# Memory keys and queries transposed inside the gate chunk, head queries behind the values, branch rows split earlier

## The reference

```python
for i in range(DEPTH):
    h = rmsnorm(x, norm_in[i])
    z = h @ w_in                       # queries, keys, values, q_mem, gate
    mix = mla_mixer(...) if i % 2 == 0 else swa_mixer(...)
    mem_o = memory_attention(q_mem, mem, ...)   # 4 heads of 128
    branch = concatenate([mix, mem_o]) * silu(gate)    # 1024 + 512 wide
    x = x + branch @ w_out[i]
```

## Time and profile before

| | |
|---|---|
| median of 3 runs | 1450.37 us (1449.27 to 1455.12) |
| the profiled execution | 1454.06 us, span 1452.3 us |
| TensorE busy | 1399.7 us, 96% |
| VectorE busy | 982.6 us, 68% |
| ScalarE busy | 760.7 us, 52% |
| GpSimd busy | 412.5 us, 28% |
| DMA | 121.47 MB, mean 84 GB/s |
| mean granted TensorE clock | 0.995 |

### The profile page before, as it was taken

One profiled execution on the slowest core, in us unless ns is written; L12 is line 12 of the kernel. 1 busy time (PEld: TensorE's weight loads), 2 busy tenths in 40 slices (PEclk: granted clock), 3 DMA queues, 4 the chain that ended last, 5 costly groups with the idle time before them and its releaser, 6 DMA issues.

```text
span 1452.3 us, 23072 instructions
## 1 busy us (share of the span) xinstructions
PE 1399.7 (96%) x8120; PEld 1242.3 (86%) x8120; DVE 982.6 (68%) x2072; ACT 760.7 (52%) x1823; POOL 412.5 (28%) x535
## 2 busy tenths in 40 slices
PE   7999999999999999999999999999999999999999
PEld 6889889898888988889878898899888888888997
DVE  6455688887755546888564657887877556477873
ACT  7354466555544436666462535656556344366651
POOL 2221342331202123645211213322311211245450
PEclk9999999999999999999999999999999999999999
DMA  6313221114341322213352132121133413122222
GB/s 231 108 47 88 82 61 53 44 47 145 127 121 50 87 63 66 69 56 97 96 194 83 45 94 82 46 61 46 37 116 116 117 44 98 57 70 62 63 72 102
DMA packets 88673, 121.47 MB, mean 84 GB/s; under 512 B 10352, under 2 KB 58864, under 8 KB 88560
## 3 DMA queue, kind: packets, MB, share of 16 engines
q1 hardware_dynamic: 83088, 112.31, 25.6%
q10 hardware_dynamic: 5472, 7.69, 1.7%
HBM read 115.77 MB, written 4.19 MB: 83 GB/s over the span
## 4 chain that ended last, share of the span: by engine, by line
PE 70%; DVE 14%; ACT 8%; issue 4%; POOL 2%; DMA 1%; SPq 1%; ACTq 0%; DVEq 0%; POOLq 0%
PE bank L1499 21%; PE bank L1501 21%; PE bank L1500 21%; PE bank L1543 5%; ACT prob L574 3%; DVE w_lo_t L873 3%; DVE bank L1260 3%; DVE probT L881 2%; POOL rr L1330 1%; ACT w_hi L549 1%; DVE gate L928 1%; PE bank L1505 1%; PE bank L1506 1%; DMA w_raw<-in_w_mem 1%; ACT q_st L571 1%
## 5 line engine op out<-in xcount | busy, mean ns | idle before, releaser
L873 DVE TENSOR_TENSOR w_lo_t<-w_raw,w_hi 128x256 fp32r<-128x256 f32 (+3 forms) x540 | 301.0, 574 | 306.1 <-ACT w_hi L549 293.8
L549 ACT ACTIVATE w_hi<-w_raw 128x256 fp32r<-128x256 f32 (+3 forms) x544 | 268.1, 510 | 353.4 <-PE bank L1501 331.3
L1499 PE MATMUL bank<-w_hi,actT 128*128 128x256 f32 (+3 forms) x1120 | 363.1, 324 | 7.3 <-DVE qT L883 3.6
L1500 PE MATMUL bank<-w_lo_t,actT 128*128 128x256 f32 (+3 forms) x1120 | 360.3, 322 | 0.0
L1499 PEld LDWEIGHTS bank<-w_hi,actT 128*128 128x128 f32 x1120 | 213.8, 191 | 23.5 <-DVE qT L883 4.1
L1500 PEld LDWEIGHTS bank<-w_lo_t,actT 128*128 128x128 f32 x1120 | 213.8, 191 | 14.3
L1383 POOL TENSOR_TENSOR prob<-prob,rinv 128x256 f32<-128x256 f32 x192 | 137.0, 744 | 302.2 <-DVE rinv L979 302.2
L1501 PE MATMUL bank<-w_hi,brlo 128*128 128x256 f32 (+1 forms) x608 | 189.1, 311 | 0.0
L574 ACT ACTIVATE prob<-bank,nmax 128x256 f32<-128x256 f32 (+2 forms) x256 | 138.3, 552 | 82.6 <-DVE nmax L1054 42.1
L1501 PE MATMUL bank<-w_hi,actT 128*128 128x512 f32 (+3 forms) x512 | 171.1, 334 | 0.0
L1499 PE MATMUL bank<-actT,w_hi 128*128 128x512 f32 x384 | 152.9, 398 | 6.2 <-DVE kT L883 5.7
(11 more groups left out here) (141 smaller groups left out, 2720.5 us busy)
## 6 DMA issues: line engine op xcount, KB each, us to landing
w_raw<-in_w_mem SPq DMA_DIRECT2D x64, 256.0 KB, 2.8
w_raw<-in_w_out SPq DMA_DIRECT2D x112, 128.0 KB, 2.1
w_raw<-in_w_b SPq DMA_DIRECT2D x112, 128.0 KB, 2.0
w_raw<-in_w_b SPq DMA_DIRECT2D x48, 256.0 KB, 2.7
w_raw<-in_w_out SPq DMA_DIRECT2D x40, 256.0 KB, 2.8
w_raw<-in_w_a SPq DMA_DIRECT2D x32, 256.0 KB, 2.7
w_raw<-in_w_a SPq DMA_DIRECT2D x64, 128.0 KB, 2.0
bias<-in_alibi ACTq DMA_DIRECT2D x28, 192.0 KB, 2.3
```

The lines of the kernel that those rows point to most:

```text
L549: act.activation(w_hi[:, n % SPLIT, 0:width], w_raw[:, n % RAW, 0:width], ACT.Copy).then_inc(w_hi_done, 1)
L873: dve.tensor_tensor(w_lo_t[:, n % SPLIT, 0:width], w_raw[:, n % RAW, 0:width], w_hi[:, n % SPLIT, 0:width].bitcast(fp32), ALU.subtract).th ...
L1499: nc.tensor.matmul(out, lhs[0], rhs[0], start=start, stop=False, skip_group_check=skip)
L1500: nc.tensor.matmul(out, lhs[0], rhs[1], start=False, stop=False, skip_group_check=skip)
```

## The change

- In all layers: `mem_keys` (transposes of the memory keys) runs inside the gate chunk behind its row 4 (`MEM_KEYS_AT`), `mem_queries` behind row 5. On ScalarE and VectorE their parts come ahead of tanh and gate tiles.
- In the even layers: ScalarE copies branch rows 8 and 9 ahead of `a_t(0)`'s parts, 10 and 11 where all four were. Each such copy of a memory row now also waits until the last gate chunk has used the row of h whose place it takes.
- In the odd layers: `FILL["b_q"]` 8 instead of 6. In the window loop TensorE does `b_q` and `b_k` behind `b_o(h)`; ScalarE does their high parts behind `b_exp(h + 2)`, VectorE the low parts behind `b_p(h + 2)`, ahead of `b_pt(h + 1)`. `WINDOW_FILL` has two steps less in heads 4 and 5, two more in head 6, two less in heads 11 and 12. The memory rows of the branch are split in heads 4 and 5.
- `plan()` follows the new order, and sets its clock 9.0 back while it takes the banks of memory keys and queries; one gap is 0.8 instead of 0.7.

```diff
-        "b_q": 6, "b_t": 2, "b_first": 3, "b_second": 3}
+        "b_q": 8, "b_t": 2, "b_first": 3, "b_second": 3}
+
+MEM_KEYS_AT = 4
...
-WINDOW_FILL = [(1, 2)] * B_BARE + [(0, 1)] + [(1, 2)] * 6 + [(1, 1)] * 2 + [(1, 0)]
+WINDOW_FILL = [(1, 2)] * 4 + [(1, 1)] * 2 + [(1, 2)] * 5 + [(1, 1)] * 4 + [(1, 0)]
...
-SPLIT_MEM_AT = {6: (8, 9), 7: (10, 11)}
+SPLIT_MEM_AT = {4: (8, 9), 5: (10, 11)}
...
-            "wide": (5.4, False, 2.0, 0.7), ...
+            "wide": (5.4, False, 2.0, 0.8), ...
...
+        clock[0] -= 9.0
         take([("memKT", L, j) for j in range(MH // 2)])
+        take([("mqT", L, 0), ("mqT", L, 1)])
+        clock[0] += 9.0
...
                 def branch_hi(j, use):
                     act.wait_ge(*read(use))
+                    if j >= MIX // P:
+                        act.wait_ge(*tile_free(CHUNKS["gate", use[1], 7][j - MIX // P]))
...
@@ ScalarE, memory stage
-                    w_hi_to(FIRST["gate", L, 1] + SPLIT)
-                    for j in range(8, 12):
-                        tanh(L, j)
-                    for j in range(MH // 2):
-                        use = ("memKT", L, j)
-                        hi(use, kT[:, 0, j, :], ...)
...
+                    w_hi_to(FIRST["gate", L, 11] + MEM_KEYS_AT + SPLIT)
+                    for j in range(MH // 2):
+                        use = ("memKT", L, j)
+                        hi(use, kT[:, 0, j, :], ...)
+                    w_hi_to(FIRST["gate", L, 11] + MEM_KEYS_AT + 1 + SPLIT)
                     mem_q(0)
                     mem_q(1)
+                    w_hi_to(FIRST["gate", L, 1] + SPLIT)
+                    for j in range(8, 12):
+                        tanh(L, j)
...
@@ ScalarE, even layer
                         fill(FILL["a_first_t"])
+                        for m in range(2):
+                            branch_hi(8 + m, ("mO", L, m))
                         a_t(0)
                         fill(FILL["a_gates"])
                         chunk_end()
-
-                        for m in range(MH):
+                        for m in range(2, MH):
                             branch_hi(8 + m, ("mO", L, m))
...
@@ ScalarE, window loop
                             fill(WINDOW_FILL[h][0])
+                            if h + 2 < HB:
+                                b_exp(h + 2)
                             if h % 2 == 0 and h + 4 < HB:
                                 b_q(h // 2 + 2)
                             if h + 3 == HB // 2:
                                 b_k(1)
-                            if h + 2 < HB:
-                                b_exp(h + 2)
                             fill(WINDOW_FILL[h][1])
...
@@ VectorE, window loop
                                 b_max(h + 2)
+                            gated(("bO", L, h), h // 2, half(h % 2))
+                            fill(WINDOW_FILL[h][1])
+                            if h + 2 < HB:
+                                b_p(h + 2)
                             if h % 2 == 0 and h + 4 < HB:
                                 b_q(h // 2 + 2)
                             if h + 3 == HB // 2:
                                 b_k(1)
-                            gated(("bO", L, h), h // 2, slice(64 * (h % 2), 64 * (h % 2) + 64))
-                            fill(WINDOW_FILL[h][1])
-                            if h + 2 < HB:
-                                b_p(h + 2)
                             if h + 1 < HB:
                                 b_pt(h + 1)
...
@@ TensorE, project
                         if k < rows - 1:
                             ins.then_inc(w_used, 1)
+                        if k in after:
+                            after[k]()
...
@@ TensorE, memory stage
+                    gate_chunk(L, 8, {MEM_KEYS_AT: mem_keys, MEM_KEYS_AT + 1: mem_queries})
...
@@ TensorE, window loop
                             if h + 2 < HB:
                                 b_s(h + 2)
+                            fill(WINDOW_FILL[h][0])
+                            b_o(h)
                             if h % 2 == 0 and h + 4 < HB:
                                 b_q(h // 2 + 2)
                             if h + 3 == HB // 2:
                                 b_k(1)
-                            fill(WINDOW_FILL[h][0])
-                            b_o(h)
                             fill(WINDOW_FILL[h][1])
```

More of the change, by code:

```diff
@@ L245, in plan @@
                     take([("bS", L, h + 2, s) for s in range(len(SHARED))])
[L246 to L249, removed]
                 if h == B_BARE:
@@ L254, in plan @@
                 take([("bO", L, h)])
+                if h % 2 == 0 and h + 4 < HB:
+                    take([("bqT", L, h // 2 + 2)])
+                if h + 3 == HB // 2:
+                    take([("bkT", L, 1)])
                 fill(stream, WINDOW_FILL[h][1])
@@ L1038, in _ @@
                          lambda i: qs_mem[:, i, :].rearrange("p (h d) -> p h d", h=MH), FIRST["gate", L, 11] + SPLIT)
-                    w_lo_to(FIRST["gate", L, 1] + SPLIT)
-                    for j in range(8, 12):
-                        gate_tile(L, j)
-                    for j in range(MH // 2):
-                        use = ("memKT", L, j)
-                        lo(use, kT[:, 1, j, :], bank(use)[:], kT[:, 0, j, :], gcol[:, GAIN_AT[f"mk{l}"]:GAIN_AT[f"mk{l}"] + 1])
                     gm = gcol[:, GAIN_AT[f"mq{l}"]:GAIN_AT[f"mq{l}"] + 1]
@@ L1058, in mem_p @@
                         over_sum([("mS", L, m, 0), ("mS", L, m, 1)], m % 2).then_inc(rinv_ready, 1)
+                    w_lo_to(FIRST["gate", L, 11] + MEM_KEYS_AT + SPLIT)
+                    for j in range(MH // 2):
+                        use = ("memKT", L, j)
+                        lo(use, kT[:, 1, j, :], bank(use)[:], kT[:, 0, j, :], gcol[:, GAIN_AT[f"mk{l}"]:GAIN_AT[f"mk{l}"] + 1])
+                    w_lo_to(FIRST["gate", L, 11] + MEM_KEYS_AT + 1 + SPLIT)
                     mem_q(0)
                     mem_q(1)
+                    w_lo_to(FIRST["gate", L, 1] + SPLIT)
+                    for j in range(8, 12):
+                        gate_tile(L, j)
                     fill(FILL["mem_q"])
@@ L1506, in mm2, with project @@
                     return nc.tensor.matmul(out, lhs, rhs[1], start=False, stop=True)
-                def project(uses, rows, operands, outs):
+                def project(uses, rows, operands, outs, after={}):
                     for k in range(rows):
@@ L1534, in tok_chunk, with gate_chunk @@
                     project(uses, KD, lambda k, j, w: (hT(k, j), w), lambda use: bank(use)[:, 0:width])
-                def gate_chunk(L, j0):
+                def gate_chunk(L, j0, after):
                     project([("gate", L, j0 + j) for j in range(4)], KD, lambda k, j, w: (cols(w, j), hT(k)),
-                            lambda use: bank(use)[:])
+                            lambda use: bank(use)[:], after)
                 def transposes(use, blocks, last=True, n=P):
@@ L1618, in _ @@
                     tok_chunk([("qmem", L, i) for i in range(NT)], MW)
-                    gate_chunk(L, 8)
-                    for j in range(NM):
-                        pe.wait_ge(*read(("memK", L, j)))
-                    for j in range(MH // 2):
-                        use = ("memKT", L, j)
-                        pe.wait_ge(*vacant(use))
-                        transposes(use, [k_mem_st[:, t, (2 * j + s) * MD:(2 * j + s + 1) * MD] for s in range(2) for t in range(NM)])
                     def mem_q(m):
@@ L1632, in mem_q, with mem_keys, mem_queries @@
                         transposes(("mqT", L, m), [qs_mem[:, i, m * MD:(m + 1) * MD] for i in range(NT)])
+                    def mem_keys():
+                        for j in range(NM):
+                            pe.wait_ge(*read(("memK", L, j)))
+                        for j in range(MH // 2):
+                            use = ("memKT", L, j)
+                            pe.wait_ge(*vacant(use))
+                            transposes(use, [k_mem_st[:, t, (2 * j + s) * MD:(2 * j + s + 1) * MD]
+                                             for s in range(2) for t in range(NM)])
+                    def mem_queries():
+                        mem_q(0)
+                        mem_q(1)
+                    gate_chunk(L, 8, {MEM_KEYS_AT: mem_keys, MEM_KEYS_AT + 1: mem_queries})
                     def mem_s(m):
@@ L1666, in mem_pv @@
                         ins.then_inc(full(use)[0], 1)
-                    mem_q(0)
-                    mem_q(1)
                     fill(FILL["mem_q"])
```

5 lines of the change are left out of this document (2 added, 3 removed).

## The result

The changed kernel takes **1487.62 us** (median; 1486.33 to 1491.49), against 1452.38 for the kernel before over all runs beside it: the ratio is 1.0248, 95% interval 1.0216 to 1.028, so 35 us are lost. The forecast was 1474 us with a range of 1445 to 1490. The time that came lies outside the likeliest case's own range (1458 to 1482); it is that of the rival in which the clock falls in every even turn (1483 to 1492), which had a chance of 0.18.

A forecast was written before the change was run, and what follows sets the result against it. The odd layers' window loop was taken as bound by a VectorE-ScalarE ring, nearly balanced with TensorE. -4.6 - 1.8 + 2 x 10.6 + 9 = +23.8 us on 1450.37 gave 1474 us, range 1445 to 1490.

The forecast's parts named there:

- likeliest case: Whole kernel: the ring lengthens the odd layers' loops, without or with some clock loss; 1458 to 1482 us, chance 0.56.
- the clock falls in every even turn: Rival, odd layers' loops: TensorE at half speed is late for the next `probT`; 1483 us and above, chance 0.18.
- part 1: Memory keys and queries inside the gate chunk, four layers: TensorE's 1.43 us wait goes; 1.15 us a layer, -4.6 us.
- part 2: Two branch rows copied before the first head transposes, two even layers: TensorE's 0.74 us wait for weights goes; -1.8 us.
- part 3: Eight filling steps before the first queries, two odd layers: 3.0 us wait shrinks to 0.65; 2.7 and 1.5 us gained.
- loops without clock: Odd layers, first to last end of `probT`: walked at 143.5 us instead of 130.2, +13.3 in the first.
- clock: Odd layers' loops: TensorE's wait once per pair of heads lowers its clock; three of 1.5 us per layer, +9 us.
- Part 4: Head queries behind the values, odd layers: both splits lie on the ring; even turns 11.0 to 11.1 us instead of 8.3.
- the ring: VectorE and ScalarE waiting on each other in the odd layers' window loop, 8.3 us a turn against TensorE's 8.2.
- TensorE's waits are what counts: Rival: the ring has unseen air and every named TensorE wait goes; 1419 us, 1425 with the ring holding part, chance 0.07.
- The new order costs the ring nothing: Rival: the splits of the moved queries overlap other waits, only the loop's start gains; 1440 us, chance 0.09.
- half is exposed: Rival: half the moved splits' cost falls on the ring, +2.2 us a layer; 1448.4, with a little clock 1450, chance 0.10.

The follow-up runs named there:

- kept_busy: The changed kernel with 9 to 18 extra TensorE matmuls ahead of the scores of heads 3, 5, 7, 9, 11 and 13; 1477.68 us, ratio 1.0154.
- keys_alone: The kernel before with only the memory keys and queries moved inside the gate chunk; 1446.23 us, ratio 0.9949.
- start_alone: The kernel before with eight filling steps before the first queries, new `WINDOW_FILL`, split branch rows, and the planner's `bqT` reading time 3.5 instead of 2.2; 1444.56 us, ratio 0.9939.
- lag_alone: The kernel before with only the planner's reading time for `bqT` at 3.5 instead of 2.2; 1452.67 us, ratio 0.9981.
- queries_alone: The kernel before with only the new order of the head queries, on the three queues and in the planner; 1506.68 us, ratio 1.0354.
- clean_back: The changed kernel with the old order of the head queries on all engines and the planner's `bqT` reading time 3.5 instead of 2.2; 1435.39 us, ratio 0.9872.
- weights_first: The changed kernel with ScalarE's weight tiles (`w_hi`) ahead of the high parts of the queries; 1462.03 us, ratio 1.0059.
- splits_early: The changed kernel, TensorE's order kept, with ScalarE's high parts ahead of the exponentials and VectorE's low parts right behind `gated`; 1443.36 us, ratio 0.9919.

## Why the prediction was right, and where its sizes were off

The direction, the place and the mechanism came as forecast; the size was forecast at +23.8 and is +35.2. Term by term:

| | forecast | traces |
|---|---|---|
| part 1, four layers | -4.6 | -7.6 |
| part 2, two layers | -1.8 | -2.1 |
| part 3, up to the first `probT` | -2.7, -1.5 | -2.65, -1.36 |
| loops without clock (143.5 walked; *kept_busy*) | +13.3, +12.1 | +19.3, +18.3 |
| clock | +9 | +11.7 |
| sum | +23.8 | +35.6 |

**Part 1** was right in kind (no wait on `kT`, no wait in the gate chunk) and too small. Up to the next matmul the transposes are 0.45 us shorter in two groups (1.58 against 2.03), where 0.35 more had been charged; the 0.3 us for late maxima did not come. The slow restart was worth 0.11 (87.30 to 87.64 against 0.23) and not 0.2. *keys_alone* shows the whole, -7.4.

**Part 2**: the 0.74 us behind the first head of L 0 is gone, and no wait for `w_lo_t` stands there. It was not run alone; 0.8 us in L 0 and 1.3 in L 2 are read from the traces.

**Part 3** was right to 0.1 us. The wait before the first queries, 3.0 us, has become

```profile
537.36 0.38 PE L1509 MATMUL bank<-w_hi,actT 128*128 128x256 f32 x1 [0.55 <-DVE w_lo_t L881]
```

against 0.65 worked out, and from 536 to 542 the clock is 1.00 (it was 0.52 behind it). What the prediction left out is that two steps less in the loop are worth 2.8 us more in the old order of the queries (*start_alone* against *lag_alone*); beside the new order they are worth 0.8 at most (156.2 in *queries_alone*, 155.4 in the kernel after), near the nothing that it said ("two steps in hand"). And it did not look at which bank the shifted planner would give to the values: alone, part 3 would have lost 12 us by that.

**Part 4**, the ring: both splits lie on it, as walked. The six even turns of L 1 are 12.6 us in the mean where *clean_back* has 9.5, 3.1 us more (2.9 in *kept_busy*), against 2.8 forecast. *weights_first* gives back ScalarE's half, *splits_early* most of both. The step that failed is the walk of the ring with TensorE always in time and every split at its usual length. The odd turns of L 1 are 9.0 us longer than walked. 5.2 of these go when the fillers keep the clock up in *kept_busy*: I had TensorE in time because its pair of turns was 16.75 us against 19.2, but a wait that ends with the low parts lets it go late and at half clock, and it is late with the values of the odd turn behind. So nearly all of the clock's price falls in the odd turns. At full clock it is late by little. 2.1 us are the three weight splits of 1.25 us beside GpSimd's work, in the kernel after too (617.24, 661.47, 684.87); the prediction asked of GpSimd only whether its earlier work would hold up VectorE in the even layers, and put nothing for it in the odd ones. 1.3 are head 3's, where *kept_busy* can't tell the bank from its fillers, and 0.3 are spread. The even turns' 2.3 us are a split of 0.98 us in head 2, the wait for `w_hi` in head 4, and for the other half not known.

**The clock.** I took six of twelve waits at 1.5 us, +9; eleven of twelve lowered the clock, at about 1.1 us each by the loops. Number and price erred against each other, so that a term of +9 beside +11.7 is in part luck. The Trainium skill ("TensorE: Matmul & The Clock Gate", section "HAM oscillation — how this bites in real kernels") tells of a wait in each pass of a loop that lowers the clock in each pass. The traces agree on how often; paid at 1.5 each that gave +18, and *kept_busy* has at least 10 to 14. That the rest is time that TensorE had in hand is likely, but not shown.

**The rivals.** That TensorE's waits are what counts (1425) fell: the named ones went, and the time rose. In *clean_back* those for `probT` grew and the time fell. The rule cited for it (the Trainium skill, "Perfetto Trace Analysis", section "Optimization Strategy", to look for the gaps of the most-contended engine) is not idle here: in the kernel before, TensorE's work seems to have set the loop's length, by the sums beside *start_alone*. It becomes wrong with the next step only, when one removes such a gap by a move that lengthens the ring just below. "The new order costs the ring nothing" (1440) and "half is exposed" (1450) do not hold with the splits where the diff puts them. With other places *splits_early* comes near the first (1443); *weights_first*, which takes half of the splits off the ring, is at 1462 and not at 1450.

**Left open**: why *splits_early* has shorter odd turns than expected, what its last 8 us beside *clean_back* are, what the clock costs in a run with all fillers in time, and whether GpSimd's work is what makes the weight splits long. No run has the new order of the queries with the planner's number at 3.5, so how much of TensorE's waits for the bank of `qT`, and of the clock behind them, another draw of banks would spare is open too. Part 2 was read from traces only.

## What to carry to other kernels

When two engines that feed each other have nearly the same length of turn as the busiest one, look where each of them idles inside the turn, and leave the small work there: moved out of such holes, 2.9 us of splits per pair of heads cost 25 to 26 us a layer (*queries_alone*), and 5 of that were left with TensorE's order kept as moved and the splits back near their holes (*splits_early* beside *clean_back*). The cost of a wait does not stop where the wait ends: follow the engine that it lets go into the next turn, at the clock that it then has. Look in the same way at an experiment: whether the work that should fill a wait ends before the wait would have. And where a planner hands out banks by assumed times, move its numbers with the work: here one number stood between a gain of 0.6% and a loss of 0.8% for the same step.

## What the runs showed of the hardware that I had not expected

- Eight transposes of 128x128, alone between matmuls, took 0.79 us up to the next matmul; sixteen in a row took 2.03. Of the change back to matmuls the trace shows 0.08 us: 0.31 instead of 0.23 between the first two.
- Two waits of nearly the same length, at the same place of two like layers, differ in what they do to the clock: 2.48 us gave 0.75 over the next 6 us, 2.47 us gave 1.00. All ten longer ones, 2.86 to 4.68 us, lowered it, and so did waits of 2.46 and 2.49 us ahead of the fillers of *kept_busy*.
- 9 to 18 idle matmuls per wait raised the mean clock of the loops from 0.89 and 0.90 to 0.98 and made the kernel 10 us faster, by its medians. Where their own bank came late, they ran at the lower clock themselves and held TensorE 1.45 us beyond the wait that they were to fill.
- A weight split of 128x256 on VectorE took 0.42 us, and 1.25 us in three places where GpSimd made a low part of the branch (1.29 us each) at the same time.
